# Two-layer hybrid decoder in float32: the second feed-forward product as seven block products in place of eight

## What is computed

```
h2 = rms_norm(x, norm2_g[l])
x = x + jnp.square(jax.nn.relu(h2 @ w_ff1[l])) @ w_ff2[l]     # 1024 -> 4096 -> 1024
```

## Time and profile before

| | |
|---|---|
| time, median of 3 runs | 1796.24 us (1796.21 to 1796.32) |
| span of the profiled execution | 1793.5 us; no time of its own is listed beside it |
| instructions | 26458 |
| TensorE busy | 1776.8 us, 10078 matmuls and transposes |
| VectorE, ScalarE, GpSimd busy | 856.7, 466.6, 1030.1 us |
| feed-forward of layer 0 | from about 549 to 899 us of the span |

### The profile page before, as it was taken

How to read it: one execution, slowest core, us unless ns; L and a number is a source line. 1 busy time by engine, 2 the same in 40 slices (tenths; PEclk the granted TensorE clock), 3 DMA queues, 4 the chain that set the end, 5 groups by cost and what they waited for, 6 DMA issues and landing times.

```text
span 1793.5 us, 26458 instructions
## 1 busy us (share of the span) xinstructions
PE 1776.8 (99%) x10078; PEld 1449.8 (81%) x10078; DVE 856.7 (48%) x1436; ACT 466.6 (26%) x922; POOL 1030.1 (57%) x580
## 2 busy tenths in 40 slices
PE   8999999999999999999999999999999999999999
PEld 7777888788888888888877788887888888888887
DVE  8786626644444231314276964466435351414141
ACT  6423317641113000000155142266311130001011
POOL 6543466255666666666664435652556666666663
PEclk9999999999999999999999999999999999999999
DMA  6222132132333333333342212320323333333332
GB/s 233 94 71 72 58 96 94 36 118 83 94 94 109 101 99 94 94 101 99 94 141 71 83 49 73 104 83 26 128 89 100 94 94 94 97 103 94 94 96 80
DMA packets 48439, 167.25 MB, mean 93 GB/s; under 512 B 5136, under 2 KB 10544, under 8 KB 47824
## 3 DMA queue, kind: packets, MB, share of 16 engines
q1 hardware_dynamic: 47024, 156.42, 28.1%
q10 hardware_dynamic: 1312, 9.33, 1.4%
HBM read 159.44 MB, written 6.29 MB: 92 GB/s over the span
## 4 chain that ended last, share of the span: by engine, by line
PE 94%; DVE 3%; ACT 2%; issue 1%; DMA 0%; SPq 0%; DVEq 0%; ACTq 0%
PE ps L461 28%; PE ps L463 27%; PE ps L462 27%; PE ps L967 2%; PE ps L976 1%; PE ps L989 1%; DVE acc L1511 1%; DVE hLo L1504 1%; PE ps L740 1%; PE ps L727 0%; PE ps L777 0%; DMA xin<-x 0%; PE ps L1039 0%; PE ps L763 0%; PE ps L752 0%
## 5 line engine op out<-in xcount | busy, mean ns | idle before, releaser
L429 POOL TENSOR_TENSOR wLo<-wraw,wHi 128x1024 fp32r<-128x1024 f32 x288 | 721.9, 2507 | 23.9
L424 POOL TENSOR_SCALAR wHi<-wraw 128x1024 fp32r<-128x1024 f32 x288 | 308.2, 1070 | 714.1 <-PE ps L463 698.4
L461 PE MATMUL ps<-hHi,wHi 128*128 128x512 f32 x1360 | 554.0, 407 | 1.3 <-DVE convd L1633 1.3
L463 PE MATMUL ps<-hHi,wLo 128*128 128x512 f32 x1360 | 530.4, 390 | 0.0
L462 PE MATMUL ps<-hLo,wHi 128*128 128x512 f32 x1360 | 529.8, 390 | 0.0
L461 PEld LDWEIGHTS ps<-hHi,wHi 128*128 128x128 f32 x1360 | 255.4, 188 | 61.7 <-issue 7.7
L462 PEld LDWEIGHTS ps<-hLo,wHi 128*128 128x128 f32 x1360 | 255.7, 188 | 55.4 <-issue 4.6
L463 PEld LDWEIGHTS ps<-hHi,wLo 128*128 128x128 f32 x1360 | 255.2, 188 | 54.5
L461 PE MATMUL ps<-fHi,wHi 128*128 128x512 f32 x640 | 249.3, 390 | 0.0
L463 PE MATMUL ps<-fHi,wLo 128*128 128x512 f32 x640 | 249.0, 389 | 0.0
L462 PE MATMUL ps<-fLo,wHi 128*128 128x512 f32 x640 | 249.0, 389 | 0.0
(11 more groups left out here) (312 smaller groups left out, 1928.9 us busy)
## 6 DMA issues: line engine op xcount, KB each, us to landing
wraw<-stream SPq DMA_DIRECT2D x288, 512.0 KB, 3.5
out<-xT ACTq DMA_DIRECT2D x2, 2048.0 KB, 8.8
xT<-out ACTq DMA_DIRECT2D x2, 2048.0 KB, 8.6
xin<-x SPq DMA_DIRECT2D x4, 512.0 KB, 6.6
out<-ost SPq DMA_DIRECT2D x2, 512.0 KB, 3.0
out<-ost SPq DMA_DIRECT2D x3, 256.0 KB, 2.2
prm<-params ACTq DMA_DIRECT2D x1, 647.0 KB, 4.0
prm<-params SPq DMA_DIRECT2D x1, 576.0 KB, 8.9
```

The lines of the kernel that those rows point to most:

```text
L424: nc.gpsimd.tensor_scalar(wHi[:, slot], wraw[:, slot % RAW], 1.0, 0.0, ALU.mult, ALU.add).then_inc(unit_high, 1)
L429: nc.gpsimd.tensor_tensor(wLo[:, slot], wraw[:, slot % RAW], wHi[:, slot].bitcast(F32), ALU.subtract).then_inc(unit_split, 1)
L461: mm(o, lh[lc], rh[rc], start=start, stop=False)
L463: return mm(o, ll[lc], rh[rc], start=False, stop=stop)
```

## The change

The first product stays in tiles of 128 channels. The second is cut into eight groups of four tiles. In a group the activations are a matrix of 512 tokens x 512 channels, cut into 2 x 2 blocks of 256 x 256, and the weights one of 512 x 1024, cut into 2 x 2 blocks ("corners") of 256 x 512, each of which is one loaded unit. One level of Strassen's scheme in Winograd's form makes the product from seven block products p1 to p7, of sums and differences of blocks.

- **TensorE.** A product (`corner`) has 12 matmuls: 2 blocks of 128 tokens, 2 slices of 128 channels, 3 passes. The activation is now the stationary operand and 512 weight columns the moving one, so the result is token-major. Products and ff1 tiles alternate in the written order PLACES (f0 to f3 are the tiles of the next group); the last group has seven products in the order LAST_PLACES. p6, p7 and p4 are accumulated into bank pair X on top of p1, p3 into Y on top of p5, and p2 into Z over all groups; each of the two banks of a pair is waited for by itself.
- **The residual** is needed token-major: 32 transposes near the first tiles (`turn_residual`) bring it into `y`, ScalarE copies it. Between the layers 32 transposes (`turn_stream`) bring the result back; after the second layer `y` is stored as it is, without transposes.
- **Weights.** SyncE loads the four corners of a group to homes of their own. GpSimd adds two of them (`sum_upper`), VectorE makes three more sums of 128 x 1024 (T3 and T2 in `sum_lower`, T4 in `sum_corners`). In the feed-forward part ScalarE makes the high copies of all units (`high_part`), GpSimd the low parts only.
- **Activations.** The squares are ScalarE's; VectorE mixes the halves of a tile (`mix_halves`); ScalarE makes the high copies of blocks and mixes (`high_tile`), VectorE the low parts (`low_tile`).
- **Sums.** After each product but p2 VectorE adds or subtracts the bank pair, 128 tokens x 512 columns at a time, into the residual (`add_corner`), twelve additions a group.
- A few steps elsewhere that had a semaphore of their own now count on the shared `vector_step`; their order is the same.

```diff
+GROUPS, TURN = 8, 11
+LEAD = FF0 + 4
+SPLITS = LEAD + (GROUPS - 1) * TURN + 7
+FF_LOADS = LEAD + 4 * (GROUPS - 1)
+PLACES = ("p1", "f0", "p5", "p6", "f1", "p2", "p7", "f2", "p3", "p4", "f3")
+LAST_PLACES = ("p2", "p1", "p6", "p7", "p4", "p5", "p3")
...
+            def low_part(layer, group, place, source):
+                at = split_no(group, place)
+                pool.wait_ge(high_copied, layer * per.high_copied + at - LEAD + 1)
+                nc.gpsimd.tensor_tensor(wLo[:, at % RING], source, wHi[:, at % RING].bitcast(F32), ALU.subtract).then_inc(unit_split, 1)
+            def sum_upper(layer, group):
+                pool.wait_ge(w11_in, layer * per.corner_in + 16 * group + 16)
+                pool.wait_ge(w12_in, layer * per.corner_in + 16 * group + 16)
+                nc.gpsimd.tensor_tensor(b1112[:], w11[:], w12[:], ALU.add).then_inc(sum_b, 1)
...
+                def corner(group, place, kind, bank, opens, after=None):
+                    at = split_no(group, place)
+                    slot, b = at % RING, group % 2
+                    pe.wait_ge(unit_split, layer * per.unit_split + at + 1)
+                    for i in range(2):
+                        if after:
+                            pe.wait_ge(corner_added, added_count(layer, *after, i))
+                        for k in range(2):
+                            tokens, cols = np.s_[:, kind, k, i * P:(i + 1) * P], np.s_[:, slot, k * 512:(k + 1) * 512]
+                            mm(ps[:, bank + i], fHi[b][tokens], wHi[cols], start=opens and k == 0, stop=False, skip_group_check=True)
+                            mm(ps[:, bank + i], fHi[b][tokens], wLo[cols], start=False, stop=False, skip_group_check=True)
+                            last = mm(ps[:, bank + i], fLo[b][tokens], wHi[cols], start=False, stop=k == 1, skip_group_check=True)
+                        if i == 0:
+                            last.then_inc(first_done, 1)
+                    last.then_inc(unit_done, 1)
...
+                ff1(0)
+                sum_stream(2 * layer + 1)
+                turn_residual(0)
+                turn_residual(1)
+                ff1(1)
+                turn_residual(2)
+                turn_residual(3)
+                ff1(2)
+                ff1(3)
+                pe.wait_ge(residual_copied, layer * per.residual_copied + 4)
+                for g in range(GROUPS - 1):
+                    pe.wait_ge(vector_tile, vector_count(layer, 4 * g + 1, LOW_DONE))
+                    corner(g, "p1", 0, X, True, (g - 1, "p4") if g else None)
+                    ff1(4 * g + 4)
+                    pe.wait_ge(vector_tile, vector_count(layer, 4 * g + 3, LOW_MIXED))
+                    corner(g, "p5", 4, Y, True, (g - 1, "p3") if g else None)
+                    corner(g, "p6", 5, X, False, (g, "p1"))
+                    ff1(4 * g + 5)
+                    corner(g, "p2", 2, Z, g == 0)
+                    corner(g, "p7", 1, X, False, (g, "p6"))
+                    ff1(4 * g + 6)
+                    corner(g, "p3", 6, Y, False, (g, "p5"))
+                    corner(g, "p4", 3, X, False, (g, "p7"))
+                    ff1(4 * g + 7)
+                g = GROUPS - 1
+                pe.wait_ge(vector_tile, vector_count(layer, 4 * g + 3, LOW_MIXED))
+                corner(g, "p2", 2, Z, False)
+                corner(g, "p1", 0, X, True, (g - 1, "p4"))
+                corner(g, "p6", 5, X, False, (g, "p1"))
+                corner(g, "p7", 1, X, False, (g, "p6"))
+                corner(g, "p4", 3, X, False, (g, "p7"))
+                corner(g, "p5", 4, Y, True, (g - 1, "p3"))
+                if layer < DEPTH - 1:
+                    turn_stream(range(0, 4))
+                corner(g, "p3", 6, Y, False, (g, "p5"))
+                if layer < DEPTH - 1:
+                    turn_stream(range(4, KD))
...
+                def high_part(group, place, source, ready, count):
+                    at = split_no(group, place)
+                    act.wait_ge(ready, count)
+                    act.wait_ge(unit_done, layer * per.unit_done + at - RING + 1)
+                    nc.scalar.copy(wHi[:, at % RING], source).then_inc(high_copied, 1)
...
+                def high_tile(n):
+                    k, b, halves = n % 2, n // 4 % 2, bank_of(n).rearrange("p (h t) -> p h t", h=2)
+                    act.wait_ge(vector_tile, vector_count(layer, n, MIXED))
+                    if n % 4 < 2:
+                        nc.scalar.copy(cross[:, k], bank_of(n)[:, 256:])
+                        nc.scalar.copy(fHi[b][:, 0:2, k], halves).then_inc(scalar_tile, 1)
+                    else:
+                        nc.scalar.copy(fHi[b][:, 2:4, k], halves).then_inc(scalar_tile, 1)
+                        nc.scalar.copy(fHi[b][:, 4:7, k], mixed[:]).then_inc(scalar_tile, 1)
...
+                for g in range(GROUPS - 1):
+                    n = 4 * g + 4
+                    high_ff1(g, 1)
+                    square(n)
+                    high_corner(g, "p2")
+                    high_tile(n)
+                    high_corner(g, "p7")
+                    high_ff1(g, 2)
+                    square(n + 1)
+                    high_corner(g, "p3")
+                    high_tile(n + 1)
+                    high_corner(g, "p4")
+                    high_ff1(g, 3)
+                    square(n + 2)
+                    if g < GROUPS - 2:
+                        high_corner(g + 1, "p1")
+                        high_tile(n + 2)
+                        high_ff1(g + 1, 0)
+                        high_corner(g + 1, "p5")
+                    else:
+                        high_corner(g + 1, "p2")
+                        high_tile(n + 2)
+                        high_corner(g + 1, "p1")
+                        high_corner(g + 1, "p6")
+                    square(n + 3)
+                    high_corner(g + 1, "p6" if g < GROUPS - 2 else "p7")
+                    high_tile(n + 3)
+                high_corner(GROUPS - 1, "p4")
+                high_corner(GROUPS - 1, "p5")
+                high_corner(GROUPS - 1, "p3")
...
+                def mix_halves(n):
+                    k, bank = n % 2, bank_of(n)
+                    dve.wait_ge(scalar_tile, scalar_count(layer, n, SQUARED))
+                    if n % 4 < 2:
+                        tt_(bank[:, 256:], bank[:, 0:256], second[:, k], ALU.subtract).then_inc(vector_tile, 1)
+                        return
+                    if n >= 3:
+                        dve.wait_ge(vector_tile, vector_count(layer, n - 1 if k else n - 3, LOW_MIXED))
+                    tt_(mixed[:, 0], bank[:, 256:], second[:, k], ALU.subtract).then_inc(vector_step, 1)
+                    stt(mixed[:, 1], bank[:, 256:], -1.0, cross[:, k], ALU.mult, ALU.subtract).then_inc(vector_step, 1)
+                    steps.next()
+                    dve.wait_ge(vector_step, steps.next())
+                    stt(mixed[:, 2], bank[:, 0:256], -1.0, mixed[:, 1], ALU.mult, ALU.subtract).then_inc(vector_tile, 1)
+                def low_tile(n):
+                    k, b, halves = n % 2, n // 4 % 2, bank_of(n).rearrange("p (h t) -> p h t", h=2)
+                    kinds = np.s_[:, 0:2, k] if n % 4 < 2 else np.s_[:, 2:4, k]
+                    dve.wait_ge(scalar_tile, scalar_count(layer, n, HIGH_DONE))
+                    tt_(fLo[b][kinds], halves, fHi[b][kinds].bitcast(F32), ALU.subtract).then_inc(vector_tile, 1)
+                    if n % 4 >= 2:
+                        dve.wait_ge(scalar_tile, scalar_count(layer, n, HIGH_MIXED))
+                        tt_(fLo[b][:, 4:7, k], mixed[:], fHi[b][:, 4:7, k].bitcast(F32), ALU.subtract).then_inc(vector_tile, 1)
+                def sum_lower(group):
+                    dve.wait_ge(w22_in, layer * per.corner_in + 16 * group + 16)
+                    dve.wait_ge(sum_b, layer * per.sum_b + group + 1)
+                    tt_(w12[:], w12[:], w22[:], ALU.add).then_inc(sums_done, 1)
+                    dve.wait_ge(sums_done, sums_count(layer, group, T3))
+                    dve.wait_ge(unit_split, layer * per.unit_split + split_no(group, "p1") + 1)
+                    tt_(w11[:], w11[:], w12[:], ALU.add).then_inc(sums_done, 1)
+                def sum_corners(group):
+                    dve.wait_ge(unit_split, layer * per.unit_split + split_no(group, "p2") + 1)
+                    dve.wait_ge(sums_done, sums_count(layer, group, T2))
+                    tt_(w21[:], w21[:], w11[:], ALU.add).then_inc(sums_done, 1)
+                def add_corner(group, place, bank, row, half, op, since=None):
+                    cols = np.s_[half * 512:(half + 1) * 512]
+                    for i in range(2):
+                        if since:
+                            dve.wait_ge(corner_added, added_count(layer, *since, i))
+                        if i:
+                            dve.wait_ge(unit_done, layer * per.unit_done + split_no(group, place) + 1)
+                        else:
```

(34 more changed lines are left out.)

## The result

| | before | after |
|---|---|---|
| time, median of 8 runs each | 1796.28 us | 1801.8 us (1800.67 to 1803.62) |
| span of the profiled execution | 1793.5 us | 1799.5 us |
| granted clock, mean of the span | 1.00 | 0.994 |

After / before is 1.003, with a 95% interval of 1.002 to 1.0041: slower by 0.3%, 4.5 us above the point forecast and inside its range. The point stood for no change that can be told; slower held 0.39 of the chance, the largest share of the three.

The account below looks back on a forecast made before the run. TensorE's number of matmuls was taken as the bound. From a span of 1793.5 us, gains of 47.5 and the added stalls, transposes and clock summed to 1794.6, plus 2.7 to the median: 1797.3 us, range 1778 to 1812.

Parts of the forecast that it names:

- end of layer 1: After layer 1's last matmul: without the closing transposes and the copy after them, 4.0 us gained.
- first group's p6: First group of each layer: T2, its copy and low part end after the covering work; 0.5 us a layer, 1.0 lost.
- What bounds and what is removed: Feed-forward part: only the number of matmuls on TensorE sets the time; 192 fewer at 0.227 us gain 43.5 us.
- The price of sharing: VectorE operations with two SBUF inputs don't run beside GpSimd: sums end 1.07 or 0.81 us after the GpSimd operation they meet.
- The chain that decides a group: Steady groups: VectorE's chain to f3's last low part ends at 14.6 us; p5 waits 1.1 us, 13.2 over 12 groups.
- The last group: Last group of each layer: p2 waits for f3's low parts and TensorE stands 8.9 us, 17.8 in two layers.
- Transposes at the head: Start of each layer's feed-forward: 32 residual transposes cost 3.7 us a layer, 7.4; little else is lost.
- Between the layers: From layer 0's last product to the next norm's sum: transposes and a norm paced by ScalarE cost 6.5 us.
- Clock: Behind the last group's 8.9 us stalls: slow matmuls, bounded by nothing and 10.9 us; a quarter, 2.7 us, was taken.
- the third rival: The clock stays down after the long stalls: full 10.9 us in place of 2.7, 1805.5 us; chance 0.12.
- no further meeting: Judges the rival that one more VectorE-GpSimd meeting, 2.26 us, stands in 14 chains: 1829 us, half of it 1813; chance 0.14.
- the first rival: The chain fits: GpSimd doesn't go between T3 and T2, so p5's waits vanish; 1774.4 us, chance 0.26.

Follow-up runs that it names:

- e2_short_low: The kernel after, but GpSimd makes the feed-forward weights' low parts over 64 of 1024 columns only (output incomplete): 1781.45 us.
- e3_order: The kernel after, all work kept, T2 and T4 moved behind f3's low parts on VectorE, p6's copy behind that tile's on ScalarE: 1781.44 us.
- e4_few_turns: The kernel after, with 48 of the 64 residual transposes in two layers left out (output incomplete): 1799.53 us.
- e6_early_low: The kernel after, with VectorE making the next norm's first two low parts ahead of the last product's additions at the end of layer 0: 1798.71 us.
- e1_fill: The kernel after, with TensorE running 34 useless matmuls during its wait before the last group's p2: 1798.34 us.
- e7_all: The kernel after with the order edits of e5_p1_first and e6_early_low together: 1771.64 us.
- e5_p1_first: e3_order with product p1 put ahead of p2 in the last group: 1774.64 us.

## Why the prediction was right or wrong, point by point

All terms are for the span, whose prediction was 1794.6 and which came out at 1799.5.

| term | predicted | measured in the kernel after |
|---|---|---|
| 192 matmuls fewer | -43.5 | -43.5 (0.227 apart, counts as stated) |
| end of layer 1 | -4.0 | -4.0 |
| p5's wait, 12 groups | +13.2 | +14.2 (12 x 1.18: 42.0 against 40.8) |
| first group's p6 | +1.0 | +0.8 |
| last group's p2 | +17.8 | +17.4 |
| transposes at the head | +7.4 | +7.0 |
| between the layers | +6.5 | +9.3 (17.9 against 8.5) |
| clock | +2.7 | +3.8 |
| sum | +1.1 | +5.0 |

The span grew by 6.0. Of the 1.0 that the table leaves, 0.55 is there before the first feed-forward tile (549.60 against 549.05), where nothing of the second product has run; 0.45 I cannot assign.

- **What bounds and what is removed**: right. Waits for the most part, and transposes, took the gain.
- **The price of sharing**: right. 1.08 and 0.81 us after the GpSimd operation, and the one that waits goes next, as the earlier trace rows had it. e2_short_low shows the cause, e3_order that it mattered only where the rectification stood behind it. The Trainium skill, page "SBUF — State Buffer", section "Who interferes with whom", says that a VectorE instruction with two SBUF inputs contends with a GpSimd instruction that reads SBUF; the trace agrees: 3.41 us for T3 beside GpSimd, 1.22 for a sum of the same size without.
- **The chain that decides a group**: right in its order and to 0.1 us a group in its length. The restart after a wait (0.3 us) was put a little low.
- **The last group**: right, 8.5 of wait and 0.2 of restart for 8.9.
- **Transposes at the head**: right as a sum. "Little is lost" behind the copies was right too, but the covered wait is near: e4_few_turns shows 1.2 us of it.
- **Between the layers**: this is the step that failed, by 2.8 us of the 4.9. "ScalarE paces the norm: 1.65 us a slice when it doesn't wait" took its condition as given. It waits once, 3.24 us, because the additions of p3 stand ahead of the first low part in VectorE's queue and themselves wait for TensorE. I had followed ScalarE's queue and not the one that feeds it. e6_early_low took 3.1 us back with that alone.
- **Clock**: right in kind, low in size, and the row that it leaned on was misread. I took a quarter of the bound between the earlier trace rows and the rival; it was a third (3.8 of 10.9). e1_fill shows the cause. The nearest row, the 5.2 us wait at the start of the program, was taken to show no fall, because its window says 1.00. The transposes behind that wait say otherwise; sixteen of them take 3.37 us, where sixteen took 1.75 in the earlier trace rows:

```profile
5.24 3.37 PE L475 MATMUL ps<-cst,xin 128*128 128x128 f32 x16 [5.24 <-DMA xin<-x]
```

They start 0.21 us apart up to 8.22 us and 0.11 from there, and the trace's record of the granted clock begins only at 8.19 us, so that the 1.00 says nothing of the time ahead of it. Read so, the row speaks for a fall, and prices it at some 1.4 us a stall (fourteen steps, 2.98 us in place of 1.54). The argument that it gave against the third rival falls away with it; that the term came out as near as 2.7 for 3.8 owes something to luck. The rule of the Trainium skill that the prediction names (page "TensorE: Matmul & The Clock Gate", section "HAM oscillation — how this bites in real kernels"), that a long enough gap makes the next burst start cold, held in both layers behind the 8.53 us; that the clock would stay down for two products, the rival's price, did not: eight and ten steps. The granted clock also went under 1.00 in a place that the prediction excluded, between the layers (0.50 from 906 to 908).

- **Rivals**: the chain didn't fit, since GpSimd's p5 did go between T3 and T2; no further meeting stood in the chains (f2's low part took 0.95, its time alone); e3_order is the first rival made true by hand, at 1781.4 where it was priced at 1774.4. The 7.0 us between are mostly two terms that its price had too small: between the layers (2.8) and the clock (none in the price, 5.5 in the trace of e3_order), less 1.4 for a shorter wait of the last group (5.2 for 5.9 in each layer).
- **Around the span**: 2.7 us was taken from one execution to the median; now it is 2.3. In each of the eight executions of the kernel after the time is 1.8 us above its own span; the rest is scatter from one execution to another.

## What to carry to other kernels

Where an engine's queue holds work of two chains, put the operations of the chain that TensorE waits for first, and those that another engine can hold up behind them: with all work kept, moving two sums was worth 20 us here. When you price a stretch by the pace of one engine, follow the queue of the engine that feeds it too, up to what stands in front and waits. And a cover taken away or an order turned around moves the wait to the next thing that is late (a bank, a load), so a gain from covering the last wait is to be priced to there and no further.

## What the runs showed of the hardware

- **What a wait costs in clock doesn't go by its length alone.** After 8.53 us of standing eight and ten steps are slow in the kernel after, 3.8 us in two layers. After 5.03 us, in e3_order, they are thirteen and fourteen (867.39 to 872.95 is 5.56 us in place of 2.95), 5.5 us. After 2.31 us, in e7_all, the first four or five steps are at full pace and then some eight are slow, some 1.5 us a layer. After the 0.9 us waits of the twelve groups none is. So from the kernel after to e3_order the wait, cut from 8.5 to 5.0 us, gave back 0.8 us a layer less than its length. But equal waits differ as much: in e4_few_turns, again after 8.53 us, nine steps are slow in layer 0 and fourteen in layer 1 (1772.46 to 1778.53 is 6.07 us in place of 3.18). What decides between eight and fourteen no run here shows.
- **The same wait need not do it.** In six of the kernels TensorE waits 0.85, 0.20 and 1.78 us between the layers, close after one another. In the kernel after and e4_few_turns the steps behind these waits are slow, with the clock at half; in e1_fill, e2_short_low, e3_order and e5_p1_first none is.
- **An exchange between VectorE and GpSimd is regular**: T3, which meets one GpSimd subtraction, took 3.41 or 3.42 us in all fourteen groups where it does so in the kernel after, and as long at the last group of e3_order and of e7_all; a sum alone took 1.22 or 1.23.
